# GpSimd takes the inverse square root of the RMS norms: mean square plus epsilon to the power -0.5

## What is computed

```python
def rmsnorm(x, g):
    xf = x.astype(jnp.float32)
    y = xf * lax.rsqrt(jnp.mean(xf * xf, -1, keepdims=True) + EPS)
    return (y * g.astype(jnp.float32)).astype(x.dtype)

def layer(x, ...):
    h = rmsnorm(x, g_pre_mix)
    p = jnp.einsum('bld,dc->blc', h, w_in)
    ...                                   # spatial gating, short convolution, retention
    m = jnp.einsum('blc,cd->bld', jnp.concatenate([a_out, b_out, c_out], axis=-1), w_out)
    x = x + rmsnorm(m, g_post_mix)
    h = rmsnorm(x, g_pre_ffn)
    f = jax.nn.silu(h @ w_gate) * (h @ w_up)
    x = x + rmsnorm(f @ w_down, g_post_ffn)
    return x, a_vrows, new_buf, new_s.astype(x.dtype)
```

## Time and profile before

| what | value |
|---|---|
| time, median of 2 runs | 1361.87 us (1361.09 and 1362.64) |
| profiled execution, its own time | 1362.15 us |
| its span in the profile | 1360.4 us |
| TensorE's granted clock over the span | 0.995 of full |
| busy share PE / PEld / DVE / ACT / POOL | 98% / 95% / 52% / 33% / 3% |

### The profile page before, as it was taken

One profiled execution on the slowest core, in us unless ns is written; L12 is line 12 of the kernel. 1 busy time (PEld: TensorE's weight loads), 2 busy tenths in 40 slices (PEclk: granted clock), 3 DMA queues, 4 the chain that ended last, 5 costly groups with the idle time before them and its releaser, 6 DMA issues.

```text
span 1360.4 us, 24643 instructions
## 1 busy us (share of the span) xinstructions
PE 1328.7 (98%) x10681; PEld 1298.1 (95%) x10681; DVE 704.2 (52%) x874; ACT 452.3 (33%) x635; POOL 34.1 (3%) x58
## 2 busy tenths in 40 slices
PE   7999999999999999999989999999999999999997
PEld 7999998989999999999989999898999999999996
DVE  5656676495444444222486566847744444432225
ACT  5432124453222222222354412344522222222222
POOL 2000002000000000000020000010000000000000
PEclk9999999999999999999999999999999999999999
DMA  6322123222222322222352222131322322222221
GB/s 223 94 78 86 56 63 98 79 78 78 93 82 87 93 78 91 86 86 66 103 166 67 90 64 63 62 99 63 94 93 77 93 88 82 93 85 86 86 86 66
DMA packets 110463, 118.98 MB, mean 87 GB/s; under 512 B 4577, under 2 KB 107129, under 8 KB 110137
## 3 DMA queue, kind: packets, MB, share of 16 engines
q1 hardware_dynamic: 107456, 108.57, 25.1%
q0 software_dynamic: 2496, 8.27, 2.1%
q10 hardware_dynamic: 440, 1.09, 0.2%
HBM read 113.23 MB, written 4.69 MB: 87 GB/s over the span
## 4 chain that ended last, share of the span: by engine, by line
PE 88%; DVE 8%; ACT 1%; issue 1%; DMA 1%; ACTq 0%; DVEq 0%; SPq 0%
PE ps L496 28%; PE ps L498 27%; PE ps L497 27%; DVE x L1200 1%; DVE h_lo L1222 1%; DVE y L1195 1%; DVE r_post L1184 1%; DVE w_lo L1164 1%; PE ps L672 1%; PE ps L526 1%; PE ps L650 1%; DVE rn L1349 1%; PE ps L676 1%; PE ps L696 1%; DVE r_pre L1238 1%
## 5 line engine op out<-in xcount | busy, mean ns | idle before, releaser
L496 PE MATMUL ps<-h_hi,w_hi 128*128 128x272 f32 x2240 | 658.1, 294 | 14.5 <-DVE h_lo L1222 10.7
L498 PE MATMUL ps<-h_lo,w_hi 128*128 128x272 f32 x2240 | 646.9, 289 | 0.0
L497 PE MATMUL ps<-h_hi,w_lo 128*128 128x272 f32 x2240 | 644.3, 288 | 0.0
L496 PEld LDWEIGHTS ps<-h_hi,w_hi 128*128 128x128 f32 x2240 | 422.1, 188 | 24.4 <-issue 12.1
L497 PEld LDWEIGHTS ps<-h_hi,w_lo 128*128 128x128 f32 x2240 | 424.3, 189 | 2.3 <-issue 1.9
L498 PEld LDWEIGHTS ps<-h_lo,w_hi 128*128 128x128 f32 x2240 | 421.5, 188 | 0.0
L1164 DVE TENSOR_TENSOR w_lo<-w_raw,w_hi 128x1024 fp32r<-128x1024 f32 (+1 forms) x208 | 244.8, 1182 | 270.5 <-ACT w_hi L908 267.4
L908 ACT ACTIVATE w_hi<-w_raw 128x1024 fp32r<-128x1024 f32 (+1 forms) x208 | 211.8, 1022 | 234.3 <-DMA w_raw<-in_w_down 143.9
L496 PE MATMUL ps<-f_hi,w_hi 128*128 128x272 f32 x704 | 204.1, 290 | 0.0
L498 PE MATMUL ps<-f_lo,w_hi 128*128 128x272 f32 x704 | 203.1, 288 | 0.0
L497 PE MATMUL ps<-f_hi,w_lo 128*128 128x272 f32 x704 | 202.4, 287 | 0.0
(11 more groups left out here) (172 smaller groups left out, 1080.3 us busy)
## 6 DMA issues: line engine op xcount, KB each, us to landing
w_raw<-in_w_in SPq DMA_DIRECT2D x52, 512.0 KB, 3.6
w_raw<-in_w_gate SPq DMA_DIRECT2D x44, 512.0 KB, 3.5
w_raw<-in_w_up SPq DMA_DIRECT2D x44, 512.0 KB, 3.5
w_raw<-in_w_down SPq DMA_DIRECT2D x36, 512.0 KB, 3.3
w_raw<-in_w_out SPq DMA_DIRECT2D x16, 512.0 KB, 3.3
w_raw<-in_w_down SPq DMA_DIRECT2D x16, 256.0 KB, 2.6
tab<-in_table POOLq DMA_DIRECT2D x2, 1536.0 KB, 6.3
st_s<-in_state_ret POOLq DMA_DIRECT2D x8, 256.0 KB, 4.7
```

Source lines behind the costliest of these rows:

```text
L496: pe.matmul(out, wh, hi[:, cols(half)], start=begins, stop=False)
L497: pe.matmul(out, wl, hi[:, cols(half)], start=False, stop=False)
L498: mm = pe.matmul(out, wh, lo[:, cols(half)], start=False, stop=ends)
```

## The change

ACT now computes sum/D + eps (`ACT.Identity` in place of `ACT.Sqrt`, same scale and bias) into `r_pre` or `r_post`. GpSimd raises that half, 128 x 272 in place, to the power -0.5, with a two-operand instruction whose second operand is a column of -0.5 broadcast over the half. DVE no longer takes a reciprocal in these sixteen places; it waits for GpSimd's result, and in the pre norms first for its own sums of squares (`pre_acc`), which it has made earlier in its own order. PE's wait for the root of half 0 becomes a wait for the mean.

The new instructions stand in GpSimd's order where its transfers allow: the two of the first norm behind the layer's loads, the other six behind the layer's stores and ahead of the wait for `stored`. The helper `root_table`, which has ACT load its table for the root ahead of time, stays as it is.

```diff
         @block.gpsimd
+            pool.memset(power[:], -0.5).then_inc(eps_set, 1)
+            pool.wait_ge(eps_set, 3)
+
+            def inverse_root(r, half, means, n, done):
+
+                pool.wait_ge(means.sem, n)
+                rr = r[:, 0, cols(half)]
+                pool.tensor_tensor(rr, rr, over(power[:], [P, H2]), ALU.pow).then_inc(done.sem, 1)
+
+            def pre_scale(layer, norm, half):
+                inverse_root(r_pre, half, pre_mean, pre_mean.at(layer, 2 * norm + half + 1), r_pre_made)
+
+            def post_scale(layer, norm, half):
+                inverse_root(r_post, half, post_mean, post_mean.at(layer, 2 * norm + half + 1), r_post_made)
...
+                for half in range(2):
+                    pre_scale(l, 0, half)
...
+                for half in range(2):
+                    post_scale(l, 0, half)
+                for half in range(2):
+                    pre_scale(l, 1, half)
+                for half in range(2):
+                    post_scale(l, 1, half)
                 pool.wait_ge(stored.sem, stored.at(l + 1, 0))
...
         @block.scalar
-                def pre_root_half(norm, half):
+                def pre_mean_half(norm, half):
                     act.wait_ge(pre_sum.sem, pre_sum.at(l, 2 * norm + half + 1))
-                    act.activation(r_pre[:, 0, cols(half)], ps[:, 6 - 2 * half, 0:H2], ACT.Sqrt,
-                                   bias=eps[:, 0:1], scale=1.0 / D).then_inc(pre_root.sem, 1)
+                    act.activation(r_pre[:, 0, cols(half)], ps[:, 6 - 2 * half, 0:H2], ACT.Identity,
+                                   bias=eps[:, 0:1], scale=1.0 / D).then_inc(pre_mean.sem, 1)
...
         @block.vector
-            def recip_post(layer, n, y_tiles, half):
+            def post_scaled(layer, n, y_tiles, half):
 
-                vec.wait_ge(post_root.sem, post_root.at(layer, n))
-                vec.reciprocal(r_post[:, 0, cols(half)], r_post[:, 0, cols(half)]).then_inc(r_post_made.sem, 1)
                 vec.wait_ge(r_post_made.sem, r_post_made.at(layer, n))
                 vec.wait_ge(y_made.sem, y_made.at(layer, y_tiles) + 8)
...
-                def recip_pre(norm, half):
-                    vec.wait_ge(pre_root.sem, pre_root.at(l, 2 * norm + half + 1))
-                    vec.reciprocal(r_pre[:, 0, cols(half)], r_pre[:, 0, cols(half)]).then_inc(r_pre_made.sem, 1)
+                def pre_scaled(norm, half):
+                    vec.wait_ge(pre_acc.sem, pre_acc.at(l, 6 * norm + 6))
                     vec.wait_ge(r_pre_made.sem, r_pre_made.at(l, 2 * norm + half + 1))
```

More of the change, by code:

```diff
@@ L187, in build @@
         eps = sb("eps", [P, 1])
+        power = sb("power", [P, 1])
         spare = sb("spare", [P, 1])
@@ L279, in build @@
         pre_sum = signal("pre_sum", 2 * 2)
-        pre_root = signal("pre_root", 2 * 2)
+        pre_mean = signal("pre_mean", 2 * 2)
         r_pre_made = signal("r_pre_made", 2 * 2)
@@ L285, in build @@
         post_sum = signal("post_sum", 2 * 2)
-        post_root = signal("post_root", 2 * 2)
+        post_mean = signal("post_mean", 2 * 2)
         r_post_made = signal("r_post_made", 2 * 2)
@@ L540, in normed_units @@
                         if half and i == 2:
-                            pe.wait_ge(pre_root.sem, pre_root.at(layer, 2 * norm + 1))
+                            pe.wait_ge(pre_mean.sem, pre_mean.at(layer, 2 * norm + 1))
                         kh = i % 2
@@ L555, in post_sums @@
                 sum_squares(layer, post_acc, 6 * norm + 5 + half, post_sum, 2 + half, half)
-            pe.wait_ge(eps_set, 2)
+            pe.wait_ge(eps_set, 3)
             pe.wait_ge(const_landed, 16)
@@ L967, in post_half, with post_mean_half @@
                                        scale=gain_of(l, gain, k)).then_inc(y_made.sem, 1)
-                def post_root_half(norm, half):
+                def post_mean_half(norm, half):
                     act.wait_ge(post_sum.sem, post_sum.at(l, 2 * norm + half + 1))
-                    act.activation(r_post[:, 0, cols(half)], ps[:, 2 + half, 0:H2], ACT.Sqrt,
-                                   bias=eps[:, 0:1], scale=1.0 / D).then_inc(post_root.sem, 1)
+                    act.activation(r_post[:, 0, cols(half)], ps[:, 2 + half, 0:H2], ACT.Identity,
+                                   bias=eps[:, 0:1], scale=1.0 / D).then_inc(post_mean.sem, 1)
                 if l == 0:
@@ L976, in _ @@
                     act.wait_ge(prm_turned, 2)
-                    act.wait_ge(eps_set, 2)
+                    act.wait_ge(eps_set, 3)
                     act.wait_ge(x_ready, 1)
@@ L1043, in _ @@
                     if u == 2:
-                        pre_root_half(0, 0)
+                        pre_mean_half(0, 0)
                     split(l, u + LEAD)
@@ L1047, in _ @@
                     if u == 3:
-                        pre_root_half(0, 1)
+                        pre_mean_half(0, 1)
                     if u in (4, 5):
@@ L1096, in last_pair @@
                             pass_on(norm, 0, range(2, 4))
-                        post_root_half(norm, half)
+                        post_mean_half(norm, half)
                         if half == 0:
@@ L1111, in ffn_pair @@
                     if first:
-                        pre_root_half(1, 0)
+                        pre_mean_half(1, 0)
                     else:
@@ L1118, in ffn_pair @@
                         split(l, FFN0 + 5, j)
-                        pre_root_half(1, 1)
+                        pre_mean_half(1, 1)
                     for half in range(2):
@@ L1262, in last_pair @@
                             post_add(norm, 3, 0)
-                        recip_post(l, 2 * norm + half + 1, 16 * norm + 14 + 2 * half, half)
+                        post_scaled(l, 2 * norm + half + 1, 16 * norm + 14 + 2 * half, half)
                         def then_low(pair):
@@ L1399, in _ @@
                     if u in (2, 3):
-                        recip_pre(0, u - 2)
+                        pre_scaled(0, u - 2)
                         scaled_out(E[K01], 0, u - 2, win_out, win_done, 1, 1)
@@ L1565, in ffn_pair @@
                     if first:
-                        recip_pre(1, 0)
+                        pre_scaled(1, 0)
                         scaled_out(E[0], 0, 0, gate_out, gate_done, j + 1, FFN0 + 1, j)
@@ L1570, in ffn_pair @@
                         split(l, FFN0 + 5, j)
-                        recip_pre(1, 1)
+                        pre_scaled(1, 1)
                         scaled_out(E[0], 0, 1, gate_out, gate_done, j + 1, FFN0 + 1, j)
```

## The result

The changed kernel takes **2028.75 us**, median of 2 runs (2027.78 and 2029.72), against 1361.87 us: 1.489 times the time before, 95% interval 1.486 to 1.492. I had said 1432 us, in a range that ended at 1566. (The range's end was slightly misadded: 1362.15 + 203 is 1565.) The direction was right, the size was wrong by a factor of nine and a half (667 us where I had 70).

A forecast was written before the change was run, and what follows sets the result against it. PE sets the time, DVE only where PE has nothing to multiply. At Q = 6.8 us: 54.7 for twelve uncovered places, 4.8 for four covered, 10.2 for the clock, +70 us on 1362.15, giving 1432 us; range 1353 to 1566.

The forecast's parts named there:

- Q: From the end of ACT's instruction to DVE's first use of the factor; put at 6.8 us, upper end 14.5.
- The much dearer power: Rival: beyond Q = 14.5 us every place adds its full Q; at 20 us, +291, 1653 us; chance 0.17.
- the sum: Delay over the sixteen places: 12 Q - 26.9, and 4 x (Q - 5.6) more beyond 5.6 us.
- Which places pay and how much cover each has: Twelve places pay Q less 1.91 to 2.93 us; the four pre norms' halves 0 pay only beyond 5.6 us.
- break-even: The value of Q, 2.24 us, at which the change neither costs nor gains time.
- The cap of 14 us: Limit on any gain, from PE's present waits: 10.7 us for `h_lo` and 3.6 us for `x`.
- Half 0 of the pre norms: Costs nothing until Q is over 5.6 us, then Q - 5.6 at each of four places; 4.8 us in all.
- Handoffs: To GpSimd, inside Q: upper bound 0.63 us, from a store waiting for a copy; taken as 0.3 us.
- The clock: PE's clock falls in longer waits, 1.7 us each: six losses, 10 us, at Q = 6.8; twelve, 20 us, at 14.5.
- GpSimd's order: Layer 1's loads start behind the last norm's half 1 power, queue free in time; costed at nothing, at most 1 us.
- The exclusion of the two engines: Rival: GpSimd waits for DVE's three additions at half 1 of post norms; +3 us, 1435 us; chance 0.5.
- The cheap power: Rival: power as cheap as the reciprocal, so not slower; at Q = 1.5, -8.9 us, 1353 us; chance 0.10.

The follow-up runs named there:

- the product: The changed kernel with a product with -0.5 in place of the power on GpSimd: 1351.5 us against 1363.4 us, ratio 0.992.
- the run with 42 columns: Changed kernel with GpSimd taking only 42 of each half's 272 columns, ACT and DVE the others by root and reciprocal: 1439.4 us against 1363.4, ratio 1.056.
- the split: Changed kernel with GpSimd taking 136 of each half's 272 columns, ACT and DVE the others by root and reciprocal: 1681.1 us against 1363.4, ratio 1.233.

## Why the prediction was wrong

The step that failed is one factor, the length of the power inside Q: "A program of 30 such passes takes 6.5 us, one of 64 takes 13.9 us." From the clears I had taken 0.8 ns for a pass over a column, and thirty of them for a power: 24 ns a column, 6.5 us for a half. No run shows such passes, or any number of them; what the runs show is 159 ns a column, 43.7 us for a half, which in the same unit would be 200. The 64 passes that made the end of the range, Q = 14.5 us, had no row behind them either. The much dearer power was a rival at 0.17, without an upper end of its own; its example stopped at 20 us.

The other steps, by the sum's terms:

- *Which places pay and how much cover each has.* Right. At the measured Q the sum gives 652 of the 666 us, six of the sixteen places lie within 0.1 us of their term, and none is more than 2.7 us off it. Without any clock term it falls short by 13, 10 and 8 us at Q = 43.8, 22.3 and 7.3 us. Below break-even it promises too much: -17.8 us at the product's Q, where -11.9 were measured. The cap of 14 us that I set for that case is not what the gain ran into.
- *Half 0 of the pre norms.* Cover of 5.6 us, taken from the FFN for all four; it is 5.4 us at three and 6.8 at the first. 38.2 us was the term, 38.1 to 39.6 were paid, 1.1 us of each for PE's sum at the lower clock. That the first place lies nearest to its term is luck, two errors that cancel.
- *Handoffs.* I took 0.3 us for them and 0.63 as the bound, from a store that waits for DVE; they are 0.12 us. A DMA's issue is no measure for a compute instruction's start.
- *The clock.* Real, and close in size (10 us for Q = 6.8 forecast, 8 measured at 7.3), but not where I had it: I spread six losses over twelve places, while it is paid at the halves 1 of the pre norms, where PE has work without DVE as soon as it is released, and with the long wait of the changed kernel also at their halves 0 and at the end. That the total came close is partly luck. At the halves 1 of the changed kernel itself (0.3 to 2.7 us over the term) the cause was not tested; that it is the clock there too is taken over from the run with 42 columns.
- *GpSimd's order.* The loads of layer 1 start at 1025.60, right behind the power that ends at 1025.61, as forecast, and the queue is free again before the next power is due (idle 1.57 us ahead of it). Costed at nothing, cost nothing.
- *The exclusion of the two engines.* Even odds given. The powers and products start while an addition of DVE is under way, so GpSimd does not wait for it; one DVE instruction near each such start takes 0.25 us longer, and the halves 1 of the post norms cost Q - 2.93 as they would without it. It decides nothing, as said.
- *The cheap power*, the rival on the other side, is what the product shows in pure form: had a power cost what a product costs, the time would be 1351.5 us. The 1353 us of that rival's example were near by luck: they were worked out for Q = 1.5, and at the product's Q the formula gives 1344.

Against the sentence from the Trainium skill (GPSIMD Engine Reference, 3.1), which gives the time of a two-operand add of 2048 columns, from which I had estimated 0.6 us for 272: for a sum and a product the trace agrees, 0.64 us. It says nothing of a power, which takes 68 times as long, and I was right not to lean on it.

## What to carry to other kernels

An operation that no row of a profile shows has no price, and a range worked out from a guessed number of steps isn't a bound: put the instruction once into an idle stretch of the engine (nine of them changed the time by a ratio of 1.0005 here, which isn't clear of noise) and read its length, before its place in the chain is even discussed. The rest of such a forecast can be had to within 2% by taking, for each place, the time that the waiting engine has left; and a cost per column is paid in full when a value is held 128 times over, once in each partition, since partitions are free and columns aren't. With the tokens laid along the partitions the same halves would be three columns wide. DVE's reciprocal would gain as well, since it too costs by the column: 1.00 us for the 136 columns of the split, 1.59 for 230 and 1.85 for 272. Neither was tried.

## What I had not expected of the hardware

- GpSimd's power: 0.36 us and 0.159 us for each column of float32, within 1% whatever the partitions (16 or 128), the exponent (-0.5 or 2) and the second operand. A product or a sum of 272 columns takes 0.64 us.
- Unused matmuls in a 5.5 us wait of PE made the kernel 8.1 us faster, by keeping its clock up: 1439.8 to 1431.8 us.
- A handoff from ACT to GpSimd takes 0.08 us, from GpSimd to DVE 0.04 us.
- Powers that ran for 156 us beside DVE left 24 of its 25 `w_lo` at their length (1214 to 1227 ns); one, near the first power's start, took 1664. The kernel's time moved by 0.05% (interval -0.04 to 0.15%).
